# Rotary halves moved by DMA within SBUF, with the first rows in two parts and output weights in free ring slots

## The reference, cut to what matters

```python
def apply_rope(x, cos, sin):        # rope() of the MLA part is the same on 32 of 96 dims
    x1, x2 = jnp.split(x, 2, axis=-1)
    rot = jnp.concatenate([-x2, x1], axis=-1)
    return x * cos + rot * sin

q = rms_norm(q, q_norm)                                   # MLA, 8 heads of 64+32; k alike
q = concatenate([q[..., :64], rope(q[..., 64:], pos)], -1)
q = apply_rope(rms_norm_2(q, q_gain), cos, sin)           # late layers, 4 heads x 2 x 64; k alike
s_c = s_c + bias_gr[t5_bucket(d_c)]                       # NSA: bias of a bucket of the distance
mixed = concatenate([y_ssm, y_sgu, y_diff], -1);  h = h + mixed @ w_out[layer]
```

## Time and profile before

| what | value |
| --- | --- |
| runs | 2930.21, 2938.16, 2938.30 us; median 2938.16 |
| profiled execution | 2938.69 us, its span 2936.9 us |
| mean granted clock | 0.978 |
| busy | PE 96%, PEld 79%, POOL 52%, DVE 36%, ACT 25% |
| DMA | 371.25 MB, mean 126 GB/s |

### The profile page before, as it was taken

The page is one execution under the profiler, slowest core; times in us unless marked ns, Lnnn a source line. Parts: engine busy times, 40 slices in busy tenths (PEclk is TensorE's granted clock), DMA queues, the critical chain, the costliest instruction groups (busy, mean ns, idle before and its releaser), DMA issues. The chain is left out here.

```text
span 2936.9 us, 38290 instructions
## 1 busy us (share of the span) xinstructions
PE 2811.3 (96%) x14613; PEld 2334.7 (79%) x14613; DVE 1050.2 (36%) x2143; ACT 726.9 (25%) x1813; POOL 1538.4 (52%) x1663
## 2 busy tenths in 40 slices
PE   6999999999999989999999989799999998899999
PEld 3544878888878889999999976578888775788887
DVE  1026662312235510000000143836447227566372
ACT  3135772100120111111111024532112225422020
POOL 0121007777777641231281155268878663588786
PEclk8999999999999979999999999899999999999999
DMA  6170003333243249999989931243332222432321
GB/s 189 50 207 29 16 2 101 97 97 101 94 158 96 78 136 278 250 255 267 264 241 268 272 115 29 83 136 96 93 100 86 86 66 72 119 101 94 99 85 53
DMA packets 539540, 371.25 MB, mean 126 GB/s; under 512 B 31242, under 2 KB 493221, under 8 KB 538328
## 3 DMA queue, kind: packets, MB, share of 16 engines
q1 hardware_dynamic: 522000, 319.46, 38.3%
q0 software_dynamic: 10912, 32.84, 3.5%
q10 hardware_dynamic: 6440, 16.44, 1.6%
HBM read 336.73 MB, written 32.41 MB: 126 GB/s over the span
## 5 line engine op out<-in xcount | busy, mean ns | idle before, releaser
L2007 POOL TENSOR_TENSOR unit_parts<-ring,unit_parts 128x512 fp32r<-128x512 f32 x580 | 805.3, 1388 | 48.4
L2005 POOL TENSOR_SCALAR unit_parts<-ring 128x512 fp32r<-128x512 f32 x580 | 422.9, 729 | 481.2 <-PE bank L598 325.3
L596 PE MATMUL bank<-x_hi,unit_parts 128*128 128x512 f32 x1408 | 556.5, 395 | 19.3 <-DVE x L2548 10.3
L597 PE MATMUL bank<-x_lo,unit_parts 128*128 128x512 f32 x1408 | 551.1, 391 | 0.0
L598 PE MATMUL bank<-x_hi,unit_parts 128*128 128x512 f32 x1408 | 551.1, 391 | 0.0
L756 PE MATMUL bank<-arena,ring 128*128 128x160 f32 x2816 | 388.5, 301 | 4.7 <-ACT arena L1758 3.8
L756 PEld LDWEIGHTS bank<-arena,ring 128*128 128x128 f32 x2816 | 386.0, 191 | 5.4 <-ACT arena L1758 4.0
L596 PEld LDWEIGHTS bank<-x_hi,unit_parts 128*128 128x128 f32 x1408 | 266.1, 189 | 78.2 <-issue 11.7
L596 PE MATMUL bank<-unit_parts,hid_parts 128*128 128x512 f32 x784 | 308.8, 394 | 12.8 <-POOL unit_parts L2007 7.5
L598 PEld LDWEIGHTS bank<-x_hi,unit_parts 128*128 128x128 f32 x1408 | 266.1, 189 | 56.3
L597 PEld LDWEIGHTS bank<-x_lo,unit_parts 128*128 128x128 f32 x1408 | 266.0, 189 | 55.6 <-issue 1.4
(11 more groups left out here) (349 smaller groups left out, 3416.6 us busy)
## 6 DMA issues: line engine op xcount, KB each, us to landing
ring<-in_moe_w_gate SPq DMA_DIRECT2D x88, 512.0 KB, 5.8
ring<-in_moe_w_up SPq DMA_DIRECT2D x88, 512.0 KB, 7.0
ring<-in_moe_w_down SPq DMA_DIRECT2D x64, 704.0 KB, 4.9
ring<-in_w_up SPq DMA_DIRECT2D x88, 512.0 KB, 5.2
ring<-in_w_down SPq DMA_DIRECT2D x16, 1024.0 KB, 5.1
ring<-in_od_w_in SPq DMA_DIRECT2D x24, 512.0 KB, 4.6
ring<-in_ffn_w_gate SPq DMA_DIRECT2D x22, 512.0 KB, 4.0
ring<-in_ffn_w_up SPq DMA_DIRECT2D x22, 512.0 KB, 5.2
```

Of the source, the lines that this page charges most:

```text
L596: pe.matmul(ps, a[0], b[0], start=start, stop=False)
L597: pe.matmul(ps, a[0], b[1], start=False, stop=False)
L2005: pool.tensor_scalar(hi, raw, 1.0, 1.0, ALU.mult, ALU.mult).then_inc(S("units_rounded"), 1)
L2007: pool.tensor_tensor(lo, raw, hi.bitcast(F32), ALU.subtract).then_inc(S("units_split"), 1)
```

## The change

1. *Rotary by DMA.* The matrices and the rotary products on PE are gone, and the first half of each sine table has its sign turned. MLA: DVE writes the normed head to `final`; POOL issues two DMAs that copy its two 16-row halves crosswise into `rp`, then makes the cosine product on rows 64 to 96; DVE multiplies `rp` by sine in SBUF and adds. Late layers: ACT, after its Exp and after DVE's `rp2`, issues four DMAs of 32 rows that copy the halves crosswise into `final`; DVE multiplies `final` by sine in place and adds.
2. *First stage.* The row pieces of block 0 stay on ACT's queue; the other 15, the rel_bias and the bucket table go to POOL's queue; the tables go to SP's queue behind weight chunk 0. PE turns block 0 before the norm stage and the rest inside q1, where the t5 bias is now made by two products for 8 rows; the DMA to DRAM writes each row 128 times.
3. *out2.* The slot counter goes back to 0 ahead of out2's chunks, and POOL splits two units after each of merges 13, 14 and 15.
4. *Semaphores.* The loads of the second S5 half share `half1`; POOL's four clears share `pool_cleared`.

The core of the diff (lines of context and the pool_cleared edits left out):

```diff
@@ -60,7 +60,7 @@
-                  ("rotm", QK), ("rotd", P), ("bandm", T), ("bandd", T), ("cosm", T), ("sinm", T),
+                  ("bandm", T), ("bandd", T), ("cosm", T), ("sinm", T),
@@ -84,13 +84,6 @@
-    rotm, rotd = np.zeros((QK, QK)), np.zeros((P, P))
-    for m, start, half in ((rotm, 64, 16), (rotd, 0, 32), (rotd, 64, 32)):
-        for i in range(half):
-            m[start + half + i, start + i] = -1
-            m[start + i, start + half + i] = 1
-    put("rotm", rotm)
-    put("rotd", rotd)
@@ -102,10 +95,10 @@
-    put("sinm", np.concatenate([np.zeros((64, T)), np.sin(a), np.sin(a)]))
+    put("sinm", np.concatenate([np.zeros((64, T)), -np.sin(a), np.sin(a)]))
-    put("sind", np.concatenate([np.sin(a)] * 4))
+    put("sind", np.concatenate([-np.sin(a), np.sin(a)] * 2))
@@ -430,11 +422,12 @@
...
                         m = min(n - r, P - q)
-                        yield rowbuf[q:q + m, (at + r) // P, c0:c0 + w], src[r:r + m, :]
+                        yield (at + r) // P, rowbuf[q:q + m, (at + r) // P, c0:c0 + w], src[r:r + m, :]
                         r += m
...
-        rows_total = 16 * len(list(row_pieces()))
+        first_rows = [piece[1:] for piece in row_pieces() if piece[0] == 0]
+        later_rows = [piece[1:] for piece in row_pieces() if piece[0]]
@@ -798,19 +793,6 @@
-                    if 0 <= i - 2 < len(groups) and groups[i - 2]["rot"]:
-                        g = groups[i - 2]
-                        r = g["rows"]
-                        n = rope_n[0]
-                        rope_n[0] += 1
-                        ps = claim((tag, g["name"], "rot"))
-                        if g["rot"] == "m":
-                            wait_drained(pe, (tag, g["name"], "raw", 0))
-                        else:
-                            pe.wait_ge(S("heads_normed"), n - 16 + 1)
-                        src = rp[:, n % 2, :] if g["rot"] == "m" else rp2[:, n % 3, :]
-                        fill(pe.matmul(ps[0:r, :], c("rot" + g["rot"])[0:r, :], src[0:r, :],
-                                       start=True, stop=True), (tag, g["name"], "rot"))
@@ -898,24 +880,19 @@
-            pe.wait_ge(S("rows_in"), rows_total)
-            pe.wait_ge(S("consts_in"), 16)
-            for a, b in ((0, 4), (4, 5)):
+            def turn_rows(a, b):
+            pe.wait_ge(S("consts_in"), 16)
+            pe.wait_ge(S("first_rows_in"), 16 * len(first_rows))
+            turn_rows(0, 1)
-            pe.wait_ge(S("t5_in"), 1)
-            for h in range(HN):
-                for a, w in ((0, 512), (512, REV - 512)):
-                    ps = claim(("t5", h, a))
-                    fill(pe.matmul(ps[:, 0:w], relw[0:33, h, :], t5hot[0:33, a:a + w], start=True, stop=True),
-                         ("t5", h, a))
-            pe.wait_ge(S("tables_in"), 16)
@@ -928,6 +905,16 @@
+                    if name == "q1":
+                        pe.wait_ge(S("rows_in"), 16 * len(later_rows))
+                        turn_rows(1, 5)
+                        pe.wait_ge(S("rowbuf_clear"), 2)
+                        pe.wait_ge(S("rel_in"), 32)
+                        for a, w in ((0, 512), (512, REV - 512)):
+                            ps = claim(("t5", a))
+                            fill(pe.matmul(ps[0:HN, 0:w], relb[0:33, :], t5hot[0:33, a:a + w], start=True, stop=True),
+                                 ("t5", a))
+                        pe.wait_ge(S("tables_in"), 16)
@@ -1243,7 +1230,10 @@
-                    pe.wait_ge(s5_landed[f"in{a}"], 16 * (l + 1))
+                    if a:
+                        pe.wait_ge(s5_landed["half1"], half1_all * (l + 1))
+                    else:
+                        pe.wait_ge(s5_landed["in0"], 16 * (l + 1))
@@ -1254,7 +1244,8 @@
-                    pe.wait_ge(s5_landed[f"out{a}"], 16 * (l + 1))
+                    if a == 0:
+                        pe.wait_ge(s5_landed["out0"], 16 * (l + 1))
@@ -1369,6 +1360,8 @@
...
                 narrow[0] = False
+                if slot_at[0] >= SLOTS - HELD_SLOTS:
+                    slot_at[0] = 0
                 for slot in range(SLOTS - HELD_SLOTS, SLOTS):
@@ -1403,19 +1396,20 @@
-                sp.dma_start(s5_tabs[a][m], s5_dram[l, a, :, m * T:(m + 1) * T]).then_inc(s5_landed[f"tabs{a}"], 16)
+                sp.dma_start(s5_tabs[a][m], s5_dram[l, a, :, m * T:(m + 1) * T])\
+                  .then_inc(s5_landed["half1" if a else "tabs0"], 16)
-                  .then_inc(s5_landed[f"in{a}"], 16)
+                  .then_inc(s5_landed["half1" if a else "in0"], 16)
-                  .then_inc(s5_landed[f"out{a}"], 16)
+                  .then_inc(s5_landed["half1" if a else "out0"], 16)
@@ -1457,6 +1451,8 @@
+                if n == 0:
+                    sp.dma_start(cst[:, EARLY:], A["constants"][:, EARLY:]).then_inc(S("tables_in"), 16)
@@ -1476,13 +1472,10 @@
-            act.dma_start(relb[0:32, :], A["rel_bias"]).then_inc(S("rel_in"), 16)
-            act.dma_start(t5hot[0:33, :], A["t5_table"]).then_inc(S("rel_in"), 16)
-            for dst, src in row_pieces():
-                act.dma_start(dst, src).then_inc(S("rows_in"), 16)
-            act.dma_start(cst[:, EARLY:], A["constants"][:, EARLY:]).then_inc(S("tables_in"), 16)
+            for dst, src in first_rows:
+                act.dma_start(dst, src).then_inc(S("first_rows_in"), 16)
@@ -1605,12 +1598,19 @@
...
                             wait_drained(act, (tag, groups[i - 3]["name"], "raw", groups[i - 3]["raws"] - 1))
+                        swap = g["rot"] == "d"
                         ps = wait_filled(act, key)
...
                         rt_n[0] += 1
+                        if swap:
+                            act.wait_ge(S("heads_normed"), n - len(groups1) + 1)
+                            src = rp2[:, (16 + 8 * int(tag[-1]) + i - 1) % 3, :]
+                            for at, of in ((0, 32), (32, 0), (64, 96), (96, 64)):
+                                act.dma_start(g["final"][at:at + 32, :], src[of:of + 32, :])\
+                                   .then_inc(S(f"halves_swapped{i % 2}"), 16)
                     if between:
@@ -1650,15 +1650,15 @@
-            for h in range(HN):
-                for a, w in ((0, 512), (512, REV - 512)):
-                    ps = wait_filled(act, ("t5", h, a))
-                    drain(act.activation(t5rows[:, h, a:a + w], ps[:, 0:w], ACT.Copy), ("t5", h, a))
-            wait_drained(act, ("t5", HN - 1, 512))
-            act.dma_start(t5_dram.rearrange("(p n) -> p n", p=P), t5rows.rearrange("p h n -> p (h n)"))\
-               .then_inc(S("t5_out"), 16)
+                if g["name"] == "q1":
+                    for a, w in ((0, 512), (512, REV - 512)):
+                        ps = wait_filled(act, ("t5", a))
+                        drain(act.activation(t5rows[0:HN, a:a + w], ps[0:HN, 0:w], ACT.Copy), ("t5", a))
+                    wait_drained(act, ("t5", 0))
+                    wait_drained(act, ("t5", 512))
+                    act.dma_start(t5_dram.rearrange("(p h n) -> h p n", p=P, h=HN),
+                                  t5rows[0:HN, :].unsqueeze(1).broadcast_to([HN, P, REV])).then_inc(S("t5_out"), 16)
@@ -1987,6 +1987,12 @@
+            pool.wait_ge(S("rowbuf_clear"), 1)
+            pool.memset(relb[32:33, :], 1.0).then_inc(S("rowbuf_clear"), 1)
+            for dst, src in later_rows:
+                pool.dma_start(dst, src).then_inc(S("rows_in"), 16)
+            pool.dma_start(relb[0:32, :], A["rel_bias"]).then_inc(S("rel_in"), 16)
+            pool.dma_start(t5hot[0:33, :], A["t5_table"]).then_inc(S("rel_in"), 16)
@@ -2014,14 +2020,20 @@
-                        a, b = (rp[:, n % 2, :], rq) if g["rot"] == "m" else (rp2[:, n % 3, :], rq2)
-                        pool.tensor_tensor(b[0:r, n % 2, :], a[0:r, :], c("cos" + g["rot"])[0:r, :], ALU.mult)\
+                        if g["rot"] == "m":
+                            a, b, rows = g["final"], rq, slice(64, QK)
+                            for half in range(2):
+                                pool.dma_start(rp[64 + 16 * half:80 + 16 * half, n % 2, :],
+                                               a[80 - 16 * half:96 - 16 * half, :]).then_inc(S(f"mla_swapped{n % 2}"), 16)
+                        else:
+                            a, b, rows = rp2[:, n % 3, :], rq2, slice(0, P)
+                        pool.tensor_tensor(b[rows, n % 2, :], a[rows, :], c("cos" + g["rot"])[rows, :], ALU.mult)\
@@ -2344,8 +2356,9 @@
...
-                wait_filled(pool, ("mt", l, 3))
+                    if m >= 13:
+                        wait_filled(pool, ("mt", l, 3))
+                        split(f"out2_{l}", 2)
                 split(f"out2_{l}")
@@ -2367,17 +2380,14 @@
-            link(dve.memset(relb[32:33, :], 1.0))
-            dve.wait_ge(S("rel_in"), 32)
-            dve.tensor_copy(relw[0:33, :, :], relb[0:33, :].unsqueeze(2).broadcast_to([33, 8, P]))\
-               .then_inc(S("t5_in"), 1)
-            for a, n in ((0, 4), (4, 1)):
```

(36 more changed lines are left out.)

22 lines of the change are left out of this document (11 added, 11 removed).

## The result

The changed kernel is slower. Over 20 runs of each its median is 2943.85 us (2937.21 to 2956.59) against 2934.79 us (2930.21 to 2940.31) before; the ratio is 1.0036 with a 95% interval of 1.0025 to 1.0047. Forecast was 2905 with a range of 2889 to 2921. The profiled execution of the changed kernel has a span of 2941.9 us at a mean granted clock of 0.971, against 0.978 before. The sum started from 2938.2, the median of three runs; the median of the 20 is 3.4 us lower, so against a forecast change of -33.2 us stands a measured one of +9.1.

The account below looks back on a forecast made before the run. PE, busy for 96% of the span, was taken to bound the kernel. Terms of -24.0, -3.0, -5.2, -1.0 and 0 summed to -33.2 us, taking 2938.2 to 2905 us, with a range of 2889 to 2921.

Parts of the forecast that it names:

- Front: First stage: rows in two parts and two t5 products start q0 26.2 us earlier, 2.2 returned in q1: -24.0 us.
- the tables ahead of the chunks: SP's queue at the front: later weight chunks land 8.4 us later, costed at nothing, up to 4 us if PE catches up.
- MLA: MLA q/k stage: swaps replace 32 PE instructions, groups take 3.1 us, attention starts 3.7 earlier, clock returns 0.7: -3.0 us.
- X: MLA stage: time from the end of DVE's gain product to the swap's landing, 3.45 to 4.95 us, taken as 3.9.
- case C: MLA and late stages: fast swaps with k groups at PE's floor, and all late products count; 2893 us, chance 0.18.
- the clock, at which the sum had 0.7 us: MLA stage: the shorter busy stretch brings the low clock that follows somewhat forward, +0.7 us.
- rival D: Swaps queue behind weight traffic or POOL's descriptors, making the kernel slower than before; 2970 us in its example, chance 0.04.
- the sign that the forecast named for itself: Swaps: the forecast called itself wrong if a swap lands in over 5 us.
- Late rotary: Late q/k stages: eight products per layer removed, five counted, less a later tail: -2.6 per layer, -5.2 us, bounds 0 and -13.8.
- The tail itself: Last group of a late layer: DVE waits for four issues and the landing until 1853.9 instead of 1851.9; +2.5 with collision.
- out2: Start of out2: early splits give -3.9 us in layer 0 and +2.9 in layer 1; net -1.0, range -6 to +3.
- Semaphores: Joined S5 loads and POOL's clears: state_in(1) also waits for the output table; 0, at worst +2 us.

Follow-up runs that it names:

- a2: Changed kernel with the t5 table written to DRAM from 128 partitions, eight copies each, instead of 8 partitions with 128 copies each: 2938.1 us.
- c4: Changed kernel with the front as before (rows on one queue, 16 t5 products, tables on ACT's queue): 2962.7 us.
- a4: Changed kernel with MLA's rotary as products on PE again, all else kept: 2948.4 us.
- d2: The best version with MLA's rotary as products on PE: 2905.9 us.
- the best version: Changed kernel with late rotary as products, t5 write spread, first feed-forward loads held, out2 splits moved to two after merge 12, one after 13: 2895.4 us.
- a1: Changed kernel with the rotary of the two late layers as products on PE again: 2916.3 us, ratio 0.9932 to the kernel before.
- b1: Changed kernel with late rotary as products, while ACT still waits for the gain product and issues four DMAs per group into unread spare DRAM: 2925.5 us.
- d3: Changed kernel with late rotary as products, while ACT still waits for the gain product but issues no DMA: 2912.9 us.
- c1: Changed kernel with each late group's four swap DMAs shared, two issued by ACT and two by POOL ahead of its cosine: 2930.8 us.
- c2: Changed kernel with each layer's late S5 loads held on SP until the layer's last swap has landed: 2936.9 us.
- a3: Changed kernel with out2's slots and POOL's splits as before the change: 2942.8 us.
- d4: The best version with out2's slots and splits as before the change: 2904.0 us.
- d1: The best version with late swaps again, issues shared by ACT and POOL, and late S5 loads held until the last swap: 2913.3 us.

## Why the prediction was wrong

1. **Front, -24.0 forecast.** The step that brings q0 forward was right: 26.2 forecast, 26.6 in the trace. The step that failed is the sentence "the t5 table's write has eight source partitions instead of 128; its reader comes over 100 us later, 0". I asked who waits for the write and not whose transfers it slows. It cost 5.8 us (a2), and the front is worth 18.9 (c4); the two are 24.7 together, as forecast. The worry that I did price, the tables ahead of the chunks, cost nothing that any run shows.
2. **MLA, -3.0 forecast.** Its sign is right: 4.5 us in a4, not clear of noise, and 10.5 in d2 against the best version, clear of it. The landing was 1.8 us and not 2.55, so X was about 3.0 (0.15+1.03+1.8) and PE ran at its floor, 3.0 us per k group, as in case C. That the result is still near -3.0 is luck: the last swap gave back about 3 us through the contention that I had only as rival D's reason for all swaps, and the clock, at which the sum had 0.7 us, gave back more in five of ten traces. Rival D in that form did not occur, but the sign that the forecast named for itself, a swap that lands in over 5 us, came with the last MLA swap (5.2) and with the seventh of a late layer (6.9 to 8.1). (By the sum's own 8.5 us per us of X, an X of 4.95 is worth +5.9, not +5; nothing hangs on it.)
3. **Late rotary, -5.2 forecast: this is the step that decides.** It measured +26.3 in the stage and +27.5 in the time (a1): PE's waits in the two stretches grew by 32.4 us, 29.4 of them for merges, and the lower clock took about 8, against 13.8 of products saved. The sentence that failed is "the squares of the next group and the score maps queued behind; I cost that at nothing, because PE has split products in hand between two groups". The split products cover DVE's and ACT's work of the first four groups, where the gain products are at 7, 14 and 21 us as before (6.7, 13.9, 21.8). From the fifth group on, the attention steps lie between the groups, and PE's stream waits in order for a map that stands behind ACT's issues. I had named what is queued behind and not followed it to who waits for it. That ACT's issues hold the maps is shown in part, by b1 over d3 (4.9 and 5.2 us per layer with issues of 0.44 us) and by c1. The price was wrong too: 2.44 us for four issues against 1.4, by taking the pace of ACT's row loads for copies inside SBUF. A second sentence failed: "For the seven earlier groups the swap has a whole group's time". The seventh met the S5 loads, DVE waited 7.4 us for it, and PE's wait ahead of map 7 (4.9 us, 0.4 in c2) is behind that. DVE also waited 0.3 to 1.0 us for each of the first three. The tail itself, the eighth, is as forecast, 4.0 us from the gain product's end to the multiply for 4.1, with longer issues and a shorter landing.
4. **out2, -1.0 forecast.** 1.1 the other way (a3), the same within what can be measured. In the best version, with the splits one merge earlier, it is -8.6 (d4). Its two halves went as worked out: merge 15 later by 4.1 and 5.7 in a1 against forecasts of 4.2 and 4, and out2 of layer 0 started with the last values.
5. **Semaphores, 0.** No wait in the trace of the changed kernel goes to them.

The four measured terms, -18.9, -4.5, +27.5 and +1.1, make +5.2 against +9.1 for the whole, which is as close as their spreads allow.

Of the rivals, none was this one: D put "slower" on the landing of MLA's swaps, with 0.04. A rival "issues on the engine of the softmax path" could have been priced from the earlier trace rows, where POOL's four issues took 2.42 us: by my estimate four groups with attention steps times 2.4 us are 10 us per layer before any clock, and with it the sum has no gain left from that part.

The Trainium skill's rule on the shared SBUF side ("SBUF — State Buffer", section "SBUF: two separate sides") was set beside the multiply, and the trace of the changed kernel agrees with it. Ten of the 16 late multiplies took 0.68 or 0.69 us. The other six took 1.51 to 1.76, and each began while POOL's second split step, which reads SBUF too, was running:

```profile
1783.21 1.28 POOL L2013 TENSOR_TENSOR unit_parts<-ring,unit_parts 128x512 fp32r<-128x512 f32 x1
...
1783.53 1.51 DVE L2489 TENSOR_TENSOR arena<-arena,cst 128x512 f32<-128x512 f32 x1 [0.53 <-DMA arena<-arena]
```

Each of the six ended 0.5 to 0.6 us after POOL's step, and so did the three MLA multiplies that began while POOL's cosine ran: 1.30, 1.16 and, with 0.14 us of the cosine left, 0.69 us; the other 13 took 0.68 or 0.69. Before the change, with one operand in PSUM, the 16 late multiplies took 0.68 to 0.69 us. So the cosine was over in 13 of 16 cases, nearly as I had it, and the collisions came from the splits, which I hadn't looked at. They fall on the first three groups of a layer, whose gain products are on time, so they cost nothing that the landmarks show.

What stays open is how much of the longer waits for merges is issue time. b1 over d3 gives 4.9 and 5.2 us per layer with issues of 0.44 us; scaled to 0.61 us that is about 7, an estimate, of the 12.1 and 14.2. The wait behind the seventh swap is 4.9 us, but taking it away moved merge 15 by 0.8 and 1.3 only (c2). The rest is the landings in DVE's order, the product that PE no longer has ahead of a wait, and the clock, of which no run varies one alone; d1 shows that together they are enough to make the swap lose.

## What to carry to other kernels

A DMA is not free on the engine that issues it (2.44 us for four here): count issues times their time on that engine, and follow what stands behind them in its stream to the engine that waits in order for it. A broadcasting write from few partitions, or a small copy issued together with large loads, should be priced by what shares the DMA engines at that time, not by its own reader's slack. A longer wait of PE can cost twice, by itself and by a lower clock behind it (3.44 and another 2.5 us here), and work taken off PE ahead of a wait is such a longer wait; look at the clock of several executions before giving such a saving its price. Where one step of a sum moves work between engines, look first at whether the receiving engine was idle at that very place: POOL's splits gained nothing between merges 13 and 15 and 8.6 us one merge earlier.

## What the runs showed of the hardware

- Issue of a DMA by ACT: 0.61 us each for copies of 32 partitions inside SBUF (2.44 for four), 0.44 for the same source into DRAM (1.74 for four), 0.37 for the row loads at the start. When SP issued at the same time, four took 3.66. By POOL: 0.52 each for both kinds of swap.
- Landing of copies inside SBUF, from issue: 1.8 us for 32 KB on 16 partitions from POOL, 2.0 for 64 KB on 32 partitions from ACT; beside large loads 4.4 and 5.2 us (MLA) and 6.9 to 8.1 (late, layer 0).
- A 2560 KB write that reads 8 partitions made a 1 MB load land in 32.7 us in place of 5.2; the same bytes read from 128 partitions landed in 10.7 us.
- A DVE multiply with two SBUF operands, 0.68 us alone, took up to 1.76 us in the nine cases that began during a POOL instruction that reads SBUF, and ended 0.5 to 0.6 us after it in each.
- The same MLA code took 59.6 to 72.9 us in ten traces; the granted clock was 0.50 for 10 to 40 us of it in the five longest.
